# Differential attention: context and image units in turn, and the head norm's gain in the final copies

## What is computed

```python
def block(j, qb):                       # two score maps m = 0, 1 for each head h
    logits = jnp.einsum("bqhmd,bkhmd->bhmqk", qb, k).astype(jnp.float32) * scale
    p = jax.nn.softmax(logits, axis=-1)
    a = (p[:, :, 0] - lam * p[:, :, 1]).astype(v.dtype)
    return jnp.einsum("bhqk,bkhd->bqhd", a, v)
...
def finish(o, n):                       # norm over the 128 values of a head
    return (rms_norm_2(o, subln_g) * (1.0 - lambda_init)).reshape(b, n, MIX_WIDTH)

o = finish(diff_attention(q, jnp.concatenate([kc, k], axis=1),
                          jnp.concatenate([vc, v], axis=1), lam), s)
oc = finish(diff_attention(qc, kc, vc, lam), n_ctx) if need_ctx else None
...
x = x + gt[:, None] * ((o * jax.nn.silu(z)) @ w_out)
```

## Time and profile before

| what | value |
|---|---|
| median of three runs | 2897.44 us (2893.66 to 2898.96) |
| the profiled execution | 2893.18 us, span 2891.4 us |
| TensorE busy in the span | 2746.0 us, 95% |
| VectorE, ScalarE, GpSimd busy | 1589.8, 959.7, 772.0 us |
| mean granted TensorE clock | 0.986 |
| this stage, first score to last transposition's end | 2235.5 to 2437.4 us |

### The profile page before, as it was taken

One profiled execution on the slowest core, in us unless ns is written; L12 is line 12 of the kernel. 1 busy time (PEld: TensorE's weight loads), 2 busy tenths in 40 slices (PEclk: granted clock), 3 DMA queues, 4 the chain that ended last, 5 costly groups with the idle time before them and its releaser, 6 DMA issues. The chain is left out here.

```text
span 2891.4 us, 57271 instructions
## 1 busy us (share of the span) xinstructions
PE 2746.0 (95%) x23728; PEld 2064.6 (71%) x23728; DVE 1589.8 (55%) x2898; ACT 959.7 (33%) x2229; POOL 772.0 (27%) x969
## 2 busy tenths in 40 slices
PE   7989999999999999989999989999999798999999
PEld 4968788785746888744788857547887576458884
DVE  5656867864437746523662357249823774266662
ACT  2012323224421236622121258221112674122660
POOL 3312223220025500012322125135521432245000
PEclk9999999999999999999999999999999899999999
DMA  6230100112431121202101171021111211122100
GB/s 233 79 131 24 42 18 3 48 35 88 160 110 36 59 103 60 89 30 103 59 33 55 59 260 35 30 79 59 59 59 63 99 59 59 66 72 88 74 2 29
DMA packets 108419, 205.92 MB, mean 71 GB/s; under 512 B 21795, under 2 KB 26162, under 8 KB 107648
## 3 DMA queue, kind: packets, MB, share of 16 engines
q1 hardware_dynamic: 107888, 201.36, 20.0%
q0 software_dynamic: 272, 0.89, 0.1%
HBM read 186.91 MB, written 15.54 MB: 70 GB/s over the span
## 5 line engine op out<-in xcount | busy, mean ns | idle before, releaser
L712 PE MATMUL psum<-weights,h_t 128*128 128x256 f32 x1488 | 354.1, 381 | 5.5 <-ACT p_u_u L801 5.5
L712 PEld LDWEIGHTS psum<-weights,h_t 128*128 128x128 f32 x1488 | 280.7, 191 | 44.5 <-ACT p_u_u L801 6.7
L1965 PE MATMUL psum<-weights,q_l 128*128 128x512 f32 x576 | 249.7, 592 | 0.0
L1390 DVE TENSOR_REDUCE neg_max<-psum 128x1 f32<-128x768 f32 (+1 forms) x192 | 164.5, 863 | 73.2 <-PE psum L1262 53.0
L1965 PEld LDWEIGHTS psum<-weights,q_l 128*128 128x128 f32 x576 | 108.4, 190 | 130.5 <-issue 130.5
L712 PE MATMUL psum<-z_l,x_tiles 128*128 128x256 f32 x816 | 192.8, 379 | 0.5 <-POOL z_l L925 0.5
L712 PEld LDWEIGHTS psum<-z_l,x_tiles 128*128 128x128 f32 x816 | 155.2, 190 | 21.7 <-issue 0.8
L812 ACT ACTIVATE early_work<-psum 128x512 f32<-128x512 f32 (+1 forms) x80 | 45.0, 565 | 377.1 <-DVE psum L1083 247.8
L1355 ACT ACTIVATE prob<-psum,neg_max 128x768 f32<-128x768 f32 (+1 forms) x160 | 130.7, 818 | 13.8 <-DVE neg_max L1390 9.5
L1442 POOL TENSOR_TENSOR z_l<-z_l,inv_total 128x128 f32<-128x128 f32 x80 | 31.9, 399 | 385.3 <-DVE inv_total L1401 329.7
L2066 DVE TENSOR_TENSOR delta<-psum,gate 128x512 f32<-128x512 f32 x44 | 30.4, 691 | 176.0 <-PE psum L1965 176.0
(11 more groups left out here) (442 smaller groups left out, 6118.7 us busy)
## 6 DMA issues: line engine op xcount, KB each, us to landing
weights<-in_ada_w_dram SPq DMA_DIRECT2D x30, 2048.0 KB, 8.0
weights<-in_a_w_in_dram SPq DMA_DIRECT2D x10, 2048.0 KB, 8.0
weights<-in_b_w_in_dram SPq DMA_DIRECT2D x8, 2048.0 KB, 8.0
weights<-in_c_w_in_dram SPq DMA_DIRECT2D x8, 2048.0 KB, 7.8
weights<-in_w_in_dram SPq DMA_DIRECT2D x6, 2048.0 KB, 7.8
x_aside<-x_tiles SPq DMA_DIRECT2D x24, 512.0 KB, 2.6
x_tiles<-x_aside SPq DMA_DIRECT2D x4, 3072.0 KB, 14.9
weights<-in_a_w_out_dram SPq DMA_DIRECT2D x4, 2048.0 KB, 8.2
```

What stands on the lines that cost most here:

```text
L712: last = pe.matmul(dst, lhs[:, k, :], rhs[k // 2][:, k % 2, :], start=k == 0, stop=k == KH - 1)
L1390: last = dve.tensor_reduce(neg_max[:, i % 4, m:m + 1], score(i, m, 0, keys), AX, ALU.max, negate=True)
L1965: last = pe.matmul(pr.bank(4 + u % 4), m_t[:, k, P * t:P * t + P], w[:, k, :], start=(k == 0), stop=(k == KT - 1))
```

## The change

1. `diff_units` puts context and image units in turn: C, I, C, I for units 0 to 31, then 16 image units. Context heads of tiles 4 and 5 stand at the even numbers, image heads of tiles 0 and 1 at the odd ones.
2. The gain is loaded as one column of 128 numbers, and the twelve `gate` operations of GpSimd are gone. The six copies of the turned tiles take the column as their scale.
3. The head norm's bookkeeping follows the new order: `half_ends` lists the units after which four heads are squared, sums and roots have a place for each tile, and GpSimd begins a tile's norm four units after its last head, one operation per unit; in the last unit it may do up to five.

```diff
--- before.py
+++ after.py
@@ -3569,17 +3569,16 @@
-    units = []
-    for queries in (range(XT, NT), range(XT)):
-        keys = range(NT) if queries[0] < XT else range(XT, NT)
+    def of(queries, keys):
         kc = slice(P * keys[0], P * (keys[-1] + 1))
...
+    context, image = of(range(XT, NT), range(XT, NT)), of(range(XT), range(NT))
+    in_turn = [u for both in zip(context, image) for u in both]
+    return in_turn + image[len(context):]
...
-    order = [u["tile"] for u in units if u["head"] == 0]
+    order = [u["tile"] for u in units if u["head"] == 7]
+    half_ends = [i for i, u in enumerate(units) if u["head"] % 4 == 3]
...
-        return i // 4 if 0 <= i < n and i % 4 == 3 else None
+        return half_ends.index(i) if i in half_ends else None
...
-        gain = local("subln_gain", [P, P])
-        sums = local("sums", [P, 2, 8])
...
+        gain = local("subln_gain", [P, 1])
+        sums = local("sums", [P, NT, 8])
...
+            act.wait_ge(*gained.at(1))
             for j, t in enumerate(order):
                 act.wait_ge(*turned.at(j + 1))
-                act.activation(m_t[:, :, P * t:P * t + P], product_ps(j).rearrange("p (f t) -> p f t", f=KT), ACT.Copy)\
+                act.activation(m_t[:, :, P * t:P * t + P], product_ps(j).rearrange("p (f t) -> p f t", f=KT), ACT.Copy,
+                               scale=gain[:, 0:1])\
                     .then_inc(*moved.tick())
...
-            def gate(t, a, b):
-                z = by_head(z_s, t, a, b)
-                pool.tensor_tensor(z, z, wide(gain[:, :], 1, b - a), ALU.mult).then_inc(*gained.tick())
-
...
-            link(pool.tensor_scalar(gain[:, :], gain[:, :], 1.0 - init, None, ALU.mult))
+            pool.tensor_scalar(gain[:, :], gain[:, :], 1.0 - init, None, ALU.mult).then_inc(*gained.tick())
+            ends = [half_ends[x] for x in range(len(half_ends)) if half_of(x)[1]]
+            j, step = 0, 0
             for i in range(n):
                 do_ratio(i)
-                if i < 2 * NT:
-                    gate(order[i // 2], 4 * (i % 2), 4 * (i % 2) + 4)
-                j, step = divmod(i - 11, 8)
...
+                left = 5 if i == n - 1 else 1
+                while left and j < len(order) - 1 and i >= ends[j] + 4:
...
-            sync.dma_start(gain[:, :], rows_to(pr.args["c_subln_g_2"][0], P)).then_inc(*gain_loaded.tick(16))
+            sync.dma_start(gain[:, :], pr.args["c_subln_g_2"][0].rearrange("(p o) -> p o", o=1)).then_inc(*gain_loaded.tick(16))
```

More of the change, by code:

```diff
@@ L3569, in diff_units @@
 def diff_units(q_t, k_t, v_s):
-    units = []
-    for queries in (range(XT, NT), range(XT)):
-        keys = range(NT) if queries[0] < XT else range(XT, NT)
+    def of(queries, keys):
         kc = slice(P * keys[0], P * (keys[-1] + 1))
[L3576 to L3582, removed]
+        return [dict(tile=t, head=h, keys=P * len(keys),
+                     q=[q_t[64 * m:64 * m + 64, h, P * t:P * t + P] for m in range(2)],
+                     k=[k_t[64 * m:64 * m + 64, h, kc] for m in range(2)],
+                     v=[v_s[:, k, P * h:P * h + P] for k in keys]) for t in queries for h in range(8)]
+    context, image = of(range(XT, NT), range(XT, NT)), of(range(XT), range(NT))
+    in_turn = [u for both in zip(context, image) for u in both]
+    return in_turn + image[len(context):]
 def diff_attention_stage(pr, layer, units, o_s, z_s, m_t):
@@ L3627, in half_done, with half_of @@
     def half_done(i):
-        return i // 4 if 0 <= i < n and i % 4 == 3 else None
+        return half_ends.index(i) if i in half_ends else None
+    def half_of(x):
+        return units[half_ends[x]]["tile"], units[half_ends[x]]["head"] // 4
+    sum_at, tile_at = {}, {}
+    for x in range(len(half_ends)):
+        t, second = half_of(x)
+        sum_at[x] = x + 1 + 2 * len(tile_at)
+        if second:
+            tile_at[t] = sum_at[x] + 2
     def summed_at(x):
-        return summed.at(4 * (x // 2) + 1 + x % 2)
+        return summed.at(sum_at[x])
     with pr.stage() as (block, local):
@@ L3761, in take_out @@
                         act.wait_ge(*summed_at(x - 1))
-                    act.activation(square[:, :], o_s[:, order[x // 2], WCOLS * (x % 2):WCOLS * (x % 2) + WCOLS],
+                    t, second = half_of(x)
+                    act.activation(square[:, :], o_s[:, t, WCOLS * second:WCOLS * second + WCOLS],
                                    ACT.Square, scale=down).then_inc(*squared.tick())
@@ L3865, in do_ratio @@
                     .then_inc(*ratioed.tick())
-            def gate(t, a, b):
-                z = by_head(z_s, t, a, b)
-                pool.tensor_tensor(z, z, wide(gain[:, :], 1, b - a), ALU.mult).then_inc(*gained.tick())
             def root_of(j):
[L3872 to L3875, removed]
+                t = order[j]
+                pool.wait_ge(*summed.at(tile_at[t]))
+                pool.tensor_tensor(root[:, t, :], sums[:, t, :], half[:, :], ALU.pow).then_inc(*rooted.tick())
                 pool.wait_ge(*rooted.at(2 * j + 1))
-                pool.tensor_tensor(root[:, j % 2, :], root[:, j % 2, :], keep[:, j % 2, :], ALU.mult)\
+                pool.tensor_tensor(root[:, t, :], root[:, t, :], keep[:, t, :], ALU.mult)\
                     .then_inc(*rooted.tick())
@@ L3882, in scale @@
                 o = by_head(o_s, order[j], a, b)
-                pool.tensor_tensor(o, o, wide(root[:, j % 2, a:b], 2, P), ALU.mult).then_inc(*normed.tick())
+                pool.tensor_tensor(o, o, wide(root[:, order[j], a:b], 2, P), ALU.mult).then_inc(*normed.tick())
             def product(j, a, b):
@@ L3892, in _ @@
             pool.wait_ge(*gain_loaded.at(16))
-            link(pool.tensor_scalar(gain[:, :], gain[:, :], 1.0 - init, None, ALU.mult))
+            pool.tensor_scalar(gain[:, :], gain[:, :], 1.0 - init, None, ALU.mult).then_inc(*gained.tick())
+            ends = [half_ends[x] for x in range(len(half_ends)) if half_of(x)[1]]
+            j, step = 0, 0
             for i in range(n):
                 do_ratio(i)
-                if i < 2 * NT:
-                    gate(order[i // 2], 4 * (i % 2), 4 * (i % 2) + 4)
-                j, step = divmod(i - 11, 8)
[L3899 to L3905, removed]
+                left = 5 if i == n - 1 else 1
+                while left and j < len(order) - 1 and i >= ends[j] + 4:
+                    if step == 0:
+                        root_of(j)
+                    elif step <= 2:
+                        scale(j, 4 * step - 4, 4 * step)
+                    else:
+                        product(j, 4 * step - 12, 4 * step - 8)
+                    j, step, left = j + step // 4, (step + 1) % 5, left - 1
+            assert j == len(order) - 1
             root_of(j)
```

24 lines of the change are left out of this document (11 added, 13 removed).

## The result

| | before | after |
|---|---|---|
| median of 12 runs each, us | 2897.28 (2893.66 to 2902.09) | 2902.78 (2896.65 to 2906.97) |
| ratio of after to before, 95% interval | | 1.0018 (1.001 to 1.0025) |

The kernel became 5.2 us slower (2.9 to 7.2). That is clear of no change, just short of the 0.2% line of the prediction, on the side where it gave the least, and 0.8 us outside its range.

The account below looks back on a forecast made before the run. TensorE was taken as nearly full in image steps and partly idle in context steps, both rings through TensorE and ScalarE. Unit 33 0.9 us earlier, less 0.1 for copies, gave 0.8 off the 2897.44 median: 2896.6 us, range 2890 to 2902.

Parts of the forecast that it names:

- the 0.2% line of the prediction: Versions within 0.2%, 5.8 us, count as not told apart; chances: faster 0.16, within 0.71, slower 0.13.
- scores of unit 4: Stage's start: combine at 0.48 brings unit 3 1.0 us earlier, its image scores run at half clock; unit 4 at 2250.7.
- pair: One context and one image unit in turn: 3.81 after image scores plus 2.52 after context scores, 6.33 us, 14 times.
- step with a modulation piece, more: Steps 6, 14 and 22: next scores at 4.5 us against 2.52, so 2.0 each, 6.0 in all.
- square of a context half, more: Squares after a context tile's heads stand ahead of the second image exponent: 3 x 0.55 = 1.7 us.
- square of an image half, more: Squares after image heads stand ahead of a short exponent that has time, and cost nothing.
- norm on GpSimd: Norm operations after units 19, 21, 25 and 27 delay an image combine: 4 x 0.3 = 1.2 us.
- unit 33 to unit 47: End of the stage: same units, order and engines from unit 33 on, so called unchanged.
- the first rival: The pair runs at TensorE's own limit, 6.1 us, and the norm hides: 4.4 us more gained, 2892; chance 0.17.
- the image ring: Image step's loop through TensorE and ScalarE: 1.50, 0.69, 0.49 and 1.13, together 3.81 us.
- The clock rival: Clock falls in the alternating stretch, TensorE being 78% busy; one fall costs 5 to 7 us, 2901 to 2903; chance 0.15.
- the third rival: The gain lands later as 128 elements of 4 bytes; if 2 us more, 2898.6; chance 0.1.

Follow-up runs that it names:

- after_again: The changed kernel run once more, unchanged, with a second profile; median 2900.77 us, ratio to before 1.0011.
- two_squares: The changed kernel with two places for the tile square, each square waiting for the sums of the half before the last; 2893.55 us, ratio to before 0.9988.
- after_late: The changed kernel with GpSimd's wait for the gain and its scaling moved behind ratio 6; 2900.73 us, ratio to before 1.0012.
- order_only: The changed kernel with the gain as rows and the gate operations put back, so only the new unit order; 2904.80 us, ratio to before 1.0026.
- max_first: two_squares with VectorE making the first maximum ahead of the inverse; 2894.13 us, ratio to before 0.9987.
- gain_only: The kernel before with the gain as a column scaling the copies and no gate operations, old unit order; 2890.85 us, ratio to before 0.9977.
- gain_late: gain_only with GpSimd's wait for the gain and its scaling moved behind ratio 6; 2889.12 us, ratio to before 0.9977.
- old_best: gain_late with VectorE making the first maximum ahead of the inverse, old unit order; 2884.70 us, ratio to before 0.9956.
- before_squares: The kernel before with two places for the tile square and nothing else; 2895.88 us, ratio to before 0.9995.

## Why the prediction was wrong

Its terms against after, from the timelines, distances in us from the stage's first scores:

| term | predicted | measured |
|---|---|---|
| scores of unit 4 | 15.2 | 14.23 (15.36 in after_again) |
| pair | 6.33 | 6.34 |
| step with a modulation piece, more | 2.0 each | 1.67 each |
| square of a context half, more | 0.55 each | 0.66 each |
| square of an image half, more | 0 | 0.84, 0.84, 1.59 |
| norm on GpSimd | 1.2 in all | about 0.3 in all |
| clock | none | 1.36 |
| scores of unit 32 | 112.7 | 114.90 |
| scores of unit 33 | 118.1 | 119.96 (122.45) |
| unit 33 to unit 47 | 57.24, as before | 58.29 |

The measured terms give 14.23 + 14 x 6.34 + 3 x 1.67 + 3 x 0.66 + 3.27 + 0.3 + 1.36 = 114.9. That the start came out between the two profiles is luck in part: the first `combine` does not wait for the gain as laid out, and begins 6.5 us after the first scores in both, not 7.7.

**The step that failed** is "Those after image heads stand ahead of a short exponent that has time, and cost nothing". The exponent had time for the 0.63 of the square, and two_squares shows this (3.81). It had no time for a wait that the new order makes: `square` has one place, and two halves that were four units apart now end in neighbouring units. The prediction dismissed these waits ("ended nothing in the steps shown"), which was true of before and says nothing of the new distances. With the fourth one, behind unit 33 (5.05 against 4.15), the waits are worth 0.84 + 0.84 + 1.30 + 0.90 = 3.9 us, and 1.36 more at half clock. The clock's part depends on the waits. The four profiles with them (after, after_again, after_late, order_only) show a fall 101 to 108 us after the first scores, with the third held step. Three of them have one more past the start, each with another held step: the first in after_again (0.76 in the mean from 2284 to 2291) and in order_only (0.62 from 2290 to 2299), the second in after_late (0.51 from 2312.2 to 2315.7). In two_squares and max_first, without the waits, the clock is 1.00 throughout from 2254 to 2437 and from 2252 to 2435, from behind the start to nearly the stage's end. Of the third step's 1.59 only 1.30 is the wait's: 0.29 is left in two_squares, where the same `combine` meets the same scaling.

**The pair** was right in size and in cause. That TensorE's own limit would set it, the first rival, is refuted by 6.34, and max_first shows what it takes to get shorter: 2.34 + 3.81 = 6.15. The 6.2 that the prediction called TensorE's was no limit of that engine: 3.81 of it is the image ring, and the prediction itself counts 4.9 us of TensorE's work in a pair.

**The clock rival** was right that it falls in the alternating stretch, but not in why: two_squares alternates in the same way and has no such fall. Its price was wrong too: 1.4 us for a fall there (in after at 100.8, in after_again at 45.2, in after_late at 72.7), not 5 to 7. It had reckoned with 12 us at half clock, and the fall in after is much shorter (0.66 in the mean over the 5 us from 2344, 1.00 before and behind). The longer one of order_only goes with three steps that are 3.8 us longer together, `gate` included. What the rival missed is the clock of the old order: the fall that I read in the earlier trace rows is gone in gain_only and gain_late, though old_best, also without `gate`, has it again.

**The gain.** It lands 0.6 to 1.7 us earlier as a column, not later: GpSimd waits 4.5 to 5.3 us for it in the five profiles that load a column and wait for it at the start, and 5.8 to 6.2 in the four with rows. So the third rival is refuted. The Trainium skill (DMA: Bandwidth & Descriptors, Specifications) gives 512 bytes as the smallest transfer for line rate. The 128 elements of 4 bytes land sooner than the 128 rows of 512, so no price for going below it shows here; what the elements cost by their size is not separated from their smaller sum of bytes. The copies with the column as scale cost what was said: the last takes 1.11 against 1.02. The end of the stage, from the scores of unit 47 on, is even 0.8 us shorter, since the last eight transpositions run at full clock; the prediction called it unchanged. By before_squares and gain_late (above) this is where a fall of the clock happens to stand, and not the change. After:

```profile
2445.72 1.09 PE L3740 MATMUL psum<-eye,z_l 128*128 128x128 f32 x8 [2.98 <-POOL z_l L3919]
2446.86 1.11 ACT L3797 ACTIVATE q_l<-psum,subln_gain 128x1024 f32<-128x1024 f32 x1 [2.37 <-PE psum L3740]
```

Before:

```profile
2435.38 1.97 PE L3729 MATMUL psum<-eye,z_l 128*128 128x128 f32 x8 [2.98 <-POOL z_l L3910]
2437.38 1.02 ACT L3784 ACTIVATE q_l<-psum 128x1024 f32<-128x1024 f32 x1 [3.71 <-PE psum L3729]
```

**The two parts in one sum.** The prediction set a gain against a cost and found -0.8. In the stages of the runs they are: gain alone -6.5 (203.26 to 196.81), with the 0.8 of the end in it; the new order on top of it, without the wait, +3.1 (to 199.92); the wait and its clock +4.0 or +6.4 (to 203.88 or 206.35). In all +0.6 or +3.1 by the profiles, and +3.2 to +5.2 by the three timings of this kernel or its twin after_late, whose intervals overlap. Whether the 2 us between profiles and timings are chance or sit outside the stage stays open: ahead of it some of the clock's falls come and go between executions, also of one kernel.

## What to carry to other kernels

When a change interleaves two streams of work, list for each scratch tile its producer, its reader and the distance between two uses, before and after; a wait that never ended anything is no evidence once the distance shrinks. An in-order engine passes such a wait on to everything behind it, here 1.2 us of a square into 0.8 us of every engine, and a second place cures it. Judge two edits that come together apart: here the small one gained 6.6 us and the large one alone cost 7.5.

## What the hardware showed unexpectedly

- The clock's falls are partly repeatable and tied to the order: the one 38 us after the stage's first scores is in all three profiles of the old order with `gate`, and missing in both of gain_only and gain_late; in old_best it is there again at 38.5. One held step was enough to bring a fall (1.00 until 2344, then 0.66), but not every one did. In the four profiles with the wait the third always did, the first and second in three of eight cases, the fourth never.
- Executions of one kernel differ by up to 10 us ahead of the stage with the same instructions (2235.5 and 2245.1 for before). The second has more falls of the clock on the way: 0.57 from 310 to 322 us and 0.66 from 450 to 455, where the first has 1.00. A difference of that size between two single profiles says nothing; distances within a stage repeated to 0.3 us where the clock fell alike.
- `combine` took 1.77 and not 1.02 when GpSimd's scaling of 1.04 began 0.08 us ahead of it. The loss of 0.75 is 0.2 less than the 0.96 that the scaling still had to run; in the earlier trace rows it is 0.98 (1.46 against 0.48) where `gate` had 1.19 to run, again 0.2 less. It became a loss of the stage only where something waited for the sum behind it. The Trainium skill (SBUF — State Buffer, Who interferes with whom) has such a pair exclude each other and the second to start blocked; both rows agree in that the later one took longer by nearly the rest of the earlier.
